# Second block: the forgetting and difference heads run between products of the input and latent projections, projection columns reversed, latent heads last

## The reference

```python
proj = h @ w_in[l]                                # 2212 columns:
c_q, c_kv, k_rope, dq, dk, dv, fq, fk, fv, ff = parts   # 384, 256, 32, 3 x 256, 3 x 256, 4
q = rms_norm(c_q) @ w_uq;  kv = rms_norm(c_kv) @ w_ukv  # latent heads: 8 heads, width 64 + 32 rotary
o_mla = softmax(mask(q @ k.T * s)) @ v            # 8 scores
o_diff = rms_norm((softmax(q1 @ k1.T) - lam * softmax(q2 @ k2.T)) @ v) * g   # 4 heads, 8 scores
cum = cumsum(log_sigmoid(ff + bias));  o_fox = softmax(fq @ fk.T * s + cum_q - cum_k) @ fv   # 4 scores
h = layer_norm(alpha * h + concat(o_mla, o_diff, o_fox) @ w_out)
h = layer_norm(alpha * h + mixture_of_16_experts(h))   # top 2 of 16 for each token
```

## Time and profile before

| | us |
|---|---|
| median of 3 runs (lowest, highest) | 1852.04 (1848.75, 1855.86) |
| the profiled execution, its own time | 1850.06 |
| its span, first to last instruction | 1848.3 |
| TensorE busy, share of the span | 1588.5 (86%) |
| VectorE busy | 938.5 (51%) |
| ScalarE busy | 622.3 (34%) |

### The profile page before, as it was taken

How to read it: one execution, slowest core, us unless ns; L and a number is a source line. 1 busy time by engine, 2 the same in 40 slices (tenths; PEclk the granted TensorE clock), 3 DMA queues, 4 the chain that set the end, 5 groups by cost and what they waited for, 6 DMA issues and landing times.

```text
span 1848.3 us, 18868 instructions
## 1 busy us (share of the span) xinstructions
PE 1588.5 (86%) x7511; PEld 1095.8 (59%) x7511; DVE 938.5 (51%) x1346; ACT 622.3 (34%) x879; POOL 31.5 (2%) x62
## 2 busy tenths in 40 slices
PE   2889987999699987999977875999879696799985
PEld 2677766788587765888856763333327675433331
DVE  5896666855588665654375745111026575411002
ACT  1335534344334453444333631111124371211111
POOL 2000000000000000000030000000000000000000
PEclk9999998999899997999989886999999897799998
DMA  9676355856487433765464034999975404499994
GB/s 336 227 277 204 114 168 196 312 181 224 148 298 273 140 133 114 246 198 194 162 170 158 13 116 192 410 409 409 409 307 177 137 1 185 192 410 409 409 409 192
DMA packets 149964, 427.65 MB, mean 231 GB/s; under 512 B 8105, under 2 KB 16545, under 8 KB 149873
## 3 DMA queue, kind: packets, MB, share of 16 engines
q1 hardware_dynamic: 146192, 417.43, 61.7%
q0 software_dynamic: 3456, 8.87, 1.7%
q10 hardware_dynamic: 224, 0.07, 0.0%
HBM read 425.30 MB, written 1.05 MB: 231 GB/s over the span
## 4 chain that ended last, share of the span: by engine, by line
PE 45%; DVE 7%; SPq 6%; DMA 2%; ACT 1%; issue 1%; DVEq 0%
PE gp L1978 12%; PE gp L2150 9%; PE gp L2310 8%; SPq L702 6%; PE gp L2329 4%; PE mp L2350 2%; DMA raw_more<-in_exp_w_up 2%; PE gp L2295 2%; PE mp L2169 1%; PE mp L2208 1%; PE mp L2219 1%; PE mp L2218 1%; PE mp L2227 1%; DVE stats L1573 1%; DVE wlo L1153 0%
## 5 line engine op out<-in xcount | busy, mean ns | idle before, releaser
L1226 DVE TENSOR_TENSOR wlo<-raw,whi 128x2048 fp32r<-128x2048 f32 (+1 forms) x132 | 289.5, 2193 | 223.0 <-ACT whi L803 221.9
L803 ACT ACTIVATE whi<-raw 128x2048 fp32r<-128x2048 f32 (+1 forms) x132 | 242.2, 1836 | 365.3 <-PE gp L1978 200.5
L1978 PE MATMUL gp<-whi,xt_hi 128*128 128x512 f32 (+1 forms) x800 | 317.4, 397 | 32.2 <-DVE xt_lo L1275 14.1
L1978 PE MATMUL gp<-wlo,xt_hi 128*128 128x512 f32 (+1 forms) x800 | 311.3, 389 | 0.0
L1978 PE MATMUL gp<-whi,xt_lo 128*128 128x512 f32 (+1 forms) x800 | 311.1, 389 | 0.0
L1978 PEld LDWEIGHTS gp<-whi,xt_hi 128*128 128x128 f32 x800 | 154.6, 193 | 72.6 <-DVE wlo L1226 17.7
L1978 PEld LDWEIGHTS gp<-whi,xt_lo 128*128 128x128 f32 x800 | 154.3, 193 | 31.1
L1978 PEld LDWEIGHTS gp<-wlo,xt_hi 128*128 128x128 f32 x800 | 154.7, 193 | 29.1 <-issue 0.2
L1846 DVE TENSOR_SCALAR pr<-slots,key,dg 128x128 f32<-128x128 f32 x64 | 19.3, 344 | 260.1 <-PE gp L2340 260.1
L1153 DVE TENSOR_TENSOR wlo<-raw,whi 128x2048 fp32r<-128x2048 f32 (+3 forms) x36 | 68.3, 1906 | 42.4 <-ACT whi L949 41.8
L1136 DVE SCALAR_TENSOR_TENSOR acc<-raw,cact,acc 128x1024 f32<-128x1024 f32 x69 | 88.4, 1282 | 1.5
(11 more groups left out here) (384 smaller groups left out, 2352.1 us busy)
## 6 DMA issues: line engine op xcount, KB each, us to landing
raw<-in_w_in SPq DMA_DIRECT2D x60, 1024.0 KB, 6.0
raw<-in_w_ada SPq DMA_DIRECT2D x42, 1024.0 KB, 5.4
raw_deep<-in_exp_w_down SPq DMA_DIRECT2D x36, 1024.0 KB, 16.9
raw_deep<-in_exp_w_gate SPq DMA_DIRECT2D x30, 1024.0 KB, 14.4
raw_deep<-in_exp_w_up SPq DMA_DIRECT2D x30, 1024.0 KB, 16.8
raw<-in_w_gate SPq DMA_DIRECT2D x20, 1024.0 KB, 5.2
raw<-in_w_up SPq DMA_DIRECT2D x20, 1024.0 KB, 5.2
raw<-in_w_down SPq DMA_DIRECT2D x20, 1024.0 KB, 5.0
```

The source lines that it names most:

```text
L803: act.activation(slot(whi, s % SPLIT, units, cols), slot(raw, g % RAW, units, cols), ACT.Copy).then_inc(hi_done.sem, 1)
L1226: dve.tensor_tensor(slot(wlo, s % SPLIT, units, cols), slot(raw, g % RAW, units, cols), slot(whi, s % SPLIT, units, cols).bitcast(F32), AL ...
L1978: mm = pe.matmul(gp[:, q % 2, t, 0:wide], a[:, chunk, ts], w[:, unit, c0:c0 + wide], start=first and n == 0 and m == 0, stop=last and n == ...
```

## The change

The column groups of `w_in` are read in reverse, the one of 164 columns first and the latent columns last. The job order becomes forgetting, difference, latent (`JOBS`). The loop of attention becomes a function `attend(i)` on each engine. Steps 0 to 3 are called after the products of units 6 to 9, steps 4 to 6 in and after the norm of the latents, step 7 after their turn, steps 8 to 11 after the products of units 10 to 13, and steps 12 to 23 as before in a row. The latents are turned into banks of `gp`. ScalarE takes half of the `w_ukv` results from VectorE. The pairs' difference is formed between steps 16 and 18, and the output is turned in two halves.

```diff
+IN2_COLS = [(COLS * j, min(COLS, IN2 - COLS * j)) for j in reversed(range(IN2_JOBS))]
+JOBS = [MH + 2 * DH + i for i in range(FH)] + [MH + i for i in range(2 * DH)] + list(range(MH))
+FIRST_DIFF, FIRST_MLA = FH, FH + 2 * DH
+IN_STEPS = 4
+NORM_STEPS = IN_STEPS + 3
+        latent_banks = (gp[:, 1, 0, :], gp[:, 1, 1, :], gp[:, 0, 0, :])
 # ScalarE
+                high_x(X2_IN)
+                for s in range(S2_UQ):
+                    split(s + 2)
+                    if s % 2:
+                        c, wide = IN2_COLS[s // 2]
+                        take(s // 2, pr[:, 0, c:c + wide])
+                    if s == 1:
+                        ... Exp, Exp, Ln of the forgetting gates
+                    if s >= S2_UQ - IN_STEPS:
+                        attend(s - (S2_UQ - IN_STEPS))
+                act.wait_ge(*pair_free[0].at2(l, 6))
+                act.wait_ge(*pair_free[1].at2(l, 4))
+                ... four Squares with accumulation (mla_sq)
+                attend(IN_STEPS)
+                act.wait_ge(*rv2_ready.at2(l, 1))
+                act.activation(rs[:, 0:4], rv[:, 0:4], ACT.Sqrt).then_inc(rs2_ready.sem, 1)
+                for i in range(IN_STEPS + 1, NORM_STEPS):
+                    attend(i)
+                ... high of the three latent banks
+                attend(NORM_STEPS)
+                for s in range(S2_UQ, S2_OUT):
+                    split(s + 2)
+                    ... take of w_uq; of w_ukv copies of token tile 0 to km and vm
+                    attend(NORM_STEPS + 1 + s - S2_UQ)
+                for i in range(NORM_STEPS + 1 + S2_OUT - S2_UQ, AJ + 4):
+                    attend(i)
 # VectorE
+                for s in range(S2_UQ):
+                    split2(s + 2, l)
+                    if s % 2:
+                        take(s // 2, 1, pr[:, 1, c:c + wide])
+                    if s == 1:
+                        small_parameters()
+                        forget_gates(0)
+                    if s == 2:
+                        forget_gates(1)
+                    if s == 5:
+                        forget_gates(2)
+                    if s == 7:
+                        rotate_diff()
+                    if s >= S2_UQ - IN_STEPS:
+                        attend(s - (S2_UQ - IN_STEPS))
+                    if s == 8:
+                        shared_key()
+                dve.wait_ge(*mla_sq.at2(l, 4))
+                ... variances, rv2_ready
+                attend(IN_STEPS)
+                reciprocal_root(4, rs2_ready.at2(l, 1), lk)
+                ... four scalings of the latents, mla_ready
+                for i in range(IN_STEPS + 1, NORM_STEPS):
+                    attend(i)
+                spread(X2_MLA, (2, 2, 1), (mt_hi, mt_lo), latent_banks)
+                attend(NORM_STEPS)
+                for s in range(S2_UQ, S2_OUT):
+                    split2(s + 2, l)
+                    ... take, or copies of token tile 1 to km and vm
+                    attend(NORM_STEPS + 1 + s - S2_UQ)
+                    if s == S2_UKV - 1:
+                        rotate(qm[:, :, :, MN:MQ], 1, MH, KR)
+                dve.sem_inc(km_ready.sem, 1)
+                for i in range(NORM_STEPS + 1 + S2_OUT - S2_UQ, AJ + 4):
+                    attend(i)
+                    if FIRST_MLA + 4 <= i < FIRST_MLA + 7:
+                        difference(i - (FIRST_MLA + 4))
+                spread(X2_O, (2, 2), (xt_hi, xt_lo), turned_banks)
+                difference(3)
+                spread(X2_O, (2, 2), (xt_hi, xt_lo), turned_banks, 2)
 # TensorE
+                for s in range(S2_UQ):
+                    product(s)
+                    if s == 4:
+                        ... three small matmuls (cum_done)
+                    if s >= S2_UQ - IN_STEPS:
+                        attend(s - (S2_UQ - IN_STEPS))
+                for i in range(IN_STEPS, NORM_STEPS):
+                    attend(i)
+                pe.wait_ge(*mla_ready.at2(l, 1))
+                for b in range(3):
+                    turn(latent_banks[b], pr, 2 * P * b, 2 if b < 2 else 1).then_inc(tr_done.sem, 1)
+                attend(NORM_STEPS)
+                pe.wait_ge(*ft_lo.at2(l, X2_MLA + 3))
+                for s in range(S2_UQ, S2_OUT):
+                    product(s)
+                    attend(NORM_STEPS + 1 + s - S2_UQ)
+                for i in range(NORM_STEPS + 1 + S2_OUT - S2_UQ, AJ + 4):
+                    attend(i)
+                pe.wait_ge(*o2_taken.at2(l, AJ))
+                ... turn of output banks 0 and 1
+                for s in range(S2_OUT, S2_MOE):
+                    product(s)
+                    if s == S2_OUT:
+                        pe.wait_ge(*oa_ready.at2(l, 1))
+                        ... turn of output banks 2 and 3
```

More of the change, by code:

```diff
@@ L484, in program @@
         fox_ready = counted("fox_ready", 0, 0, 1)
+        kv_taken = counted("kv_taken", 0, 0, 4)
         km_ready = counted("km_ready", 0, 0, 1)
@@ L969, in _, with attend @@
                     layer_norm_root((rv2_ready.sem, 1))
[L970 to L1003, removed]
+                def attend(i):
                     if i < AJ:
                         act.wait_ge(*t2_done.at2(l, i + 1))
-                        w = job_width(i)
+                        w = job_width(JOBS[i])
                         act.activation(qkt[0:w, i % 2, :], mp[0:w, 0, :], ACT.Copy).then_inc(t2_taken.sem, 1)
@@ new lines, in _ @@
+                turned_banks = [mp[:, b, :] for b in range(4)]
+                if l > 0:
+                    split2(0, l)
+                spread(X2_IN, (2, 2, 2, 2), (xt_hi, xt_lo), turned_banks)
+                split2(1, l)
+                for s in range(S2_UQ):
+                    split2(s + 2, l)
+                    if s % 2:
+                        c, wide = IN2_COLS[s // 2]
+                        take(s // 2, 1, pr[:, 1, c:c + wide])
[12 more added lines that the diff above has]
+                        shared_key()
@@ new lines, in _ @@
+                dve.wait_ge(*mla_sq.at2(l, 4))
+                lk(dve.tensor_scalar(rv[:, 0:2], lsum4[:, 0:2], 1.0 / CQ, EPS, ALU.mult, ALU.add))
+                dve.tensor_scalar(rv[:, 2:4], lsum4[:, 2:4], 1.0 / CKV, EPS, ALU.mult, ALU.add).then_inc(rv2_ready.sem, 1)
+                attend(IN_STEPS)
+                reciprocal_root(4, rs2_ready.at2(l, 1), lk)
+                for t in range(NT):
+                    for i, (a, b) in enumerate(((0, CQ), (CQ, CQ + CKV))):
+                        lk(dve.scalar_tensor_tensor(out=pr[:, t, a:b], in0=pr[:, t, a:b], scalar=rr[:, 2 * i + t:2 * i + t + 1],
+                                                    in1=cgc[:, a:b], op0=ALU.mult, op1=ALU.mult))
@@ L2240, in weigh, with attend @@
                     pe.matmul(mp[:, 3, HD:2 * HD], pt2[:, 2 * P:3 * P], v[:, 1, :], start=False, stop=True).then_inc(o2_done.sem, 1)
-                for i in range(AJ + 4):
+                def attend(i):
                     if 0 <= i - 1 < AJ:
@@ L2258, in _ @@
                     product(s)
+                    if s == S2_OUT:
+                        pe.wait_ge(*oa_ready.at2(l, 1))
+                        for b in range(2, 4):
+                            turn(mp[:, b, :], oa, 2 * P * b).then_inc(tr_done.sem, 1)
                 uses = [2 * sum(1 for q in range(J2_MOE) if q % 2 == p) for p in range(2)]
```

258 lines of the change are left out of this document (131 added, 127 removed).

## The result

The changed kernel took 1842.47 us (median of 8 runs, 1835.16 to 1846.6); the kernel before, on the same chip, 1856.56 (8 runs, 1847.67 to 1860.28). The ratio is 0.9931, 95% interval 0.9912 to 0.9951. The forecast of 1816 and its range, 1802 to 1835, were too low: 13 us came where 36 were expected. Of the 26 us between 1816 and 1842, 4.5 lie in the kernel before, which came out at 1856.56 where the forecast had started from 1852.04; but the ratio misses the forecast as well, which was 0.981. The same kernel in a later session came out at 0.9924 (0.9909 to 0.994).

What follows compares the result with a forecast made beforehand. It took the mixers to be bound by TensorE's work plus holes, 18.5 us a layer, cold start and drain; the replay gave 18.7 less, 18 taken per layer: 36 off 1850.06 is 1814, plus 2 for the median, 1816; range 1802 to 1835.

Steps and rivals of the forecast that it cites:

- replay: TensorE's order stepped through the first layer's mixer under the change: end at 1088.5 against 1107.2, 18.7 us less.
- no stall: Steps 0 to 3 between units 6 and 9: TensorE pays only their work, 4.5 us; other bound 2 us a step.
- rival C: Gain swallowed behind the mixer, the expert stage being bound from a fixed point: time stays 1852; chance 0.04.
- from the last weighing to the first output product: End of the mixer: about 4.1 us with the output turned in halves, 9.4 before.
- The table loads: Exp and Sqrt alternate, six loads a layer instead of four, 1.28 us each without drain; 1.3 us counted.
- The norm of the latents: Between units 9 and 10, covered by steps 4 to 6: some 6 us of new waits, bounds 3 and 10.
- Work that remains at full clock: TensorE's mixer work: input products 49.6, latent products 11.6, 20 steps of 2.28, output products 22 us.
- the low clock as a rival: Rival B: TensorE stays at 1.2 GHz from 995 until attention ends, 29 us slower a layer, 1910; chance 0.05.
- Slack of VectorE: Steps 13 to 19: difference pieces of 0.7 to 0.9 us fit in slack of 0.5 a step; 0.1 added.
- Units 10 to 13 with steps 8 to 11: Latent products 11.6, steps 9.1, VectorE's late maximum for step 12 1.7: sum 22.4 us; stall bounds 0 and 10.
- the same parts, so at least as much: Second layer's mixer gains at least the first's 18.7 us; 18 taken for each layer.
- Rival A: Stalls at every interleaved step, 29 us if all come; half leaves a gain of 9, 1834; chance 0.13 with what lies between.

Runs made afterwards that it cites:

- e10: Changed kernel with e9's three order edits plus extra matmuls in TensorE's holes (fewer ahead of step 6): 1814.73 us, ratio 0.9769.
- e11: Changed kernel with one call moved, VectorE's maximum of step 5 ahead of the root and the scalings: 1836.36 us, ratio 0.9901.
- e2: Changed kernel with extra matmuls ahead of the scores of steps 4, 5 and 6, in the norm of the latents: 1832.21 us, ratio 0.9878.
- e9: Changed kernel, order only: gates one product later, difference pieces beside steps 20 to 22, maximum of step 5 before root and scalings: 1828.02 us, ratio 0.9847.
- e3: Changed kernel with the forget gates' activations, and VectorE's use of them, one product later: 1833.91 us, ratio 0.9884.
- e7: Changed kernel with no attention steps between the input products (IN_STEPS = 0): 1861.51 us, ratio 1.0037 to the kernel before.

## Why the prediction was right in direction and wrong in size

- *Right:* the three large waits of the earlier trace rows went. The input products with steps 0 to 3 between them took 54.8 us (54.0 in the second trace) against 54.5. The replay's "no stall" held there, and unit 4 was in time in the first layer. The scalings ended within 0.9 us of the replay, the wait before step 12 was 1.95 us (1.7), the hole behind unit 14 2.45 (2.9). The rest of the program moved one for one with the mixer, so rival C is out.
- *Right by luck:* from the last weighing to the first output product it took 4.1 us, as said, but with the turn at the low clock; with the clock held it is 3.4 (e10).
- *Sums of the prediction that don't come out:* the two narrow products are 3.0 us each by its own working, not 2.65 (measured 2.7); the parts up to step 3 add up to 54.8, not 54.5; and from 1064.2 on, four products of 5.44 and the hole of 2.9 give 1088.9, not 1088.5, before any time for a first product at the low clock, which it names and for which it adds nothing.
- *The table loads:* in the changed kernel the load at 1003.35 took 1.28 us and the Sqrt started at 1004.64; that at 1006.36 was followed by its Exp at 1007.65. There is no drain of 1.38, which the Trainium skill ("ScalarE: Activation LUTs", "What ACT_TABLE_LOAD costs") adds; the measurement decides.
- *The failing step, first part:* "The norm of the latents", in its sentence "Steps 4 to 6 are over at 1008.5". I let the maximum of step 5 and TensorE's step 6 pass in 3.3 us behind the scalings, and the turn in 1.1. They took 5.8 and 2.3, because both ran at 1.2 GHz; at the full clock they would have taken 3.9 and 1.2. From unit 9 to unit 10 this cost 4.0 us against the replay in the first layer. Moving the one call that put the step there won 4.1 (e11), filling the holes won 3.2 (e2). The prediction had a bound of 10 for just this case, the clock at 0.50 in the wait; I took 6.
- *The failing step, second part:* "Work that remains at full clock". I had the low clock as a rival, as all or nothing with a chance of 0.05. It came in pieces instead: behind the wait before step 12 (step 13 took 3.3 us), in the drain (8.7 us for 7.35) and in the first output product (8.6 for 5.4). The gap between e9 and e10, 5.1 and 5.7 us a layer, is its price once the order is cured.
- *Slack of VectorE:* steps 17 to 19 took 2.6 us each for 2.28, as the pieces of the difference filled VectorE; I had 0.1 for all three and it was 1.0. In e10 steps over the same jobs are 2.28 apart.
- *Units 10 to 13 with steps 8 to 11:* 22.4 in the sum, 23.4 measured, and 23.5 with the clock held (e10). The hops between engines that the replay leaves out are a likely reason; no run shows it.
- *The second layer:* "the same parts, so at least as much" failed. A late weight unit met the table loads of the gates. The stall was 2.8 us, for which I had taken 0.7 with a bound of 3, and the low clock behind it added 1.7 to unit 4. e3 took 6.0 off.
- *Rival A* came nearer in size (half of its stalls, 1834), but not by its stalls: at steps 1 to 3 there were none, the waits before steps 5 and 6 were 2.3 each (2.2 and 3.8 in the replay), and the units of the latents had the one of 1.95 (bound 10).

What stays open: I removed the low clock with extra matmuls, and did not find an order of the real work that does it. The second layer of the changed kernel varies by 4 us between two traces with the time at the low clock; why the clock stays low for longer in one of them, nothing here shows.

## What to carry to other kernels

When work is moved to hide it, replay every engine's program call by call across the seam: the expensive place is where a long call of one engine stands ahead of the short call that releases a whole step of another. Put the call that releases work first, even when the total on its engine stays the same. Where TensorE's queue has small holes, read the granted clock stretch by stretch before assuming the full clock. A bound that was worked out for the low clock is to be weighed, not only written down. A few matmuls into an unused bank measure what it costs, and together with the cured order they took the kernel from 1856 to about 1815 us.

## What the hardware showed that I had not expected

- Holes of about 2 us were enough: beside and behind waits of 2.27 and 2.25 us the clock was 0.50 (1.2 GHz), behind one of 1.95 it was 0.50 from 1043.8 to 1047.0, and the first output product began at 0.50 after a drain with 5.0 of 7.8 us busy. But the wait of 1.57 us behind unit 14 left it at 1.00 (1083.8 to 1095).
- A full queue is not the full clock. In e7 TensorE was busy 20.40 of 20.40 us at 0.50, in attention steps alone, behind one wait of 1.95 us. The same wait in the changed kernel was followed by about 3 us of low clock. In the kernel before, steps in a full queue ran at 1.00 for 37.5 us, in e10 for 22:

```profile
1030.00:1052.00 22.00, 21.83 (x166) 1.00 0.16 52
```

- 40 extra matmuls of 128 columns a layer in e10 (two records each: 850 in the window where the changed kernel has 770) held the clock at 0.99 and 1.00 through the mixers:

```profile
939.70:1087.00 147.30, 143.89 (x850) 121.23 (x848) 98.33 (x218) 83.09 (x175) 2.73 (x5) 0.99 0.40 135
1371.10:1518.20 147.10, 143.61 (x850) 120.48 (x848) 98.23 (x219) 82.89 (x175) 0.00 (x0) 1.00 0.41 138
```
